# Decode attention: the cache pages of group B are loaded from ACT's queue, those of group A from SP's

## The chip, the cores and the metric

The kernel runs on one core of a Trainium2 chip. A core has TensorE (PE in the profile), VectorE (DVE), ScalarE (ACT), GpSimd (POOL) and SyncE (SP), each with its own stream of instructions, and 16 DMA engines that they share. Engines order themselves against each other by semaphores. The metric is the device time of one execution in microseconds. Before the change it is 2261.04 us, the median of 3 runs (2259.65 to 2265.12).

## The reference

One step of a hybrid decoder layer, for a prompt of 512 tokens and for 8 decode sequences of 4 new tokens each, with 4096 cached tokens per sequence in pages of 128. The input projection feeds three head groups: A (differential attention over a paged cache), B (sparse attention: compressed blocks, selected blocks, a window of 512) and C (matrix memory). What the change touches is the decode part of A and B, which reads the whole paged cache:

```python
past = (cache_a_kv[l][page_table].reshape(db, past_len, 2, H_A, HEAD),
        cache_b_kv[l][page_table].reshape(db, past_len, 4, DH_B), ...)
...
oa = diff_attention(qa, kv_a[:, :, 0].reshape(B, L, H_A, 2, DQ_A), kv_a[:, :, 1], q_pos, jnp.arange(L), lam)
...
kg = jax.vmap(lambda a, i: a[i])(ksb, idx).astype(jnp.float32)   # B: keys of the selected blocks
vg = jax.vmap(lambda a, i: a[i])(vsb, idx).astype(jnp.float32)   # B: their values
```

One page is 128 tokens. Of group A it holds 1024 floats per token (keys and values of 4 heads, 512 KB in all), of group B the kernel needs the 256 floats of k_sel and v_sel (128 KB). The table `page_table` says which of the 320 pages of the pool belong to a sequence, so the address of every load depends on a number that is read at run time.

## The kernel before

The program runs its stages one after the other: input projection, preparation, prompt attention, compressed branch, `decode_attend`, convolution, matrix memory, output projection. Each stage sets out its own instructions for each engine, fully unrolled in this one. The change is within `decode_attend` alone.

The stage works through 80 steps, 10 for each of the 8 sequences ("rows of the batch"). A step is `page` (4 cache pages, 512 tokens), `win` (the window of 512 cached rows) or `new` (the 4 fresh tokens). In a row they come as page 0, page 1, win, page 2, page 3, new, page 4 to page 7: 64 page steps in all. I call them P0 to P7, W and N. The four pages of a page step lie in one of four slots of the rings `pa` (group A) and `pb` (group B); page step m uses slot m % 4.

- SP, page step m: it waits until `summed` says that page step m - 4 has used its slot for the last time, reads four page numbers out of the table in SBUF into registers (L1214), and issues eight loads in turn, one of `pa` (L1218) and one of `pb` (L1220) for each page. All eight count up `loaded[m % 4]`; TensorE waits for 128 more on it. For a win step SP issues one load of 512 KB.
- TensorE is software pipelined over the steps. Its iteration n is: `score(n-1)` (keys times queries), `turn(n, 0)` and `turn(n, 1)` (transposes of the keys of heads 0 and 1 of step n into one of two PSUM buffers `tp`, L1296, the first behind the wait for the loads), `turn_p(n-2)`, the turns 2, 3 and 4 (the last is group B's), and `values(n-2)` (L1354, L1357), which counts up `summed`. A turn needs its `tp` buffer empty.
- ACT, iteration n: `copy_o(n-3)`, which waits for `summed` and copies the result of a step out of PSUM (L1460; L1462 for a win step, L1464 and L1465 for a new step), `copy_turn(n, 0)` (L1416, empties `tp`), `softmax(n-1)` (L1427, L1438), `copy_turn(n, 2)`, `copy_p(n-2)` (L1450), `copy_turn(n, 4)`. DVE empties the turns 1 and 3 (L1503).

So one iteration of ACT runs from one `copy_o` to the next, and TensorE's turns 2 and 4 can't start before ACT has emptied turn 0 and turn 2. The `copy_o` of step n-3 and SP's next loads are released by the same count of `summed`.

```python
for n in range(N + 9):
    if 3 <= n < N + 3:
        copy_o(n - 3)
    copy_turn(n, 0)
    if 1 <= n <= N:
        softmax(n - 1)
    copy_turn(n, 2)
    if 2 <= n < N + 2:
        copy_p(n - 2)
    copy_turn(n, 4)
```

Of the kernel before, what the change touches and what calls it, by code (L numbers as in the profile page):

```python
# [30 lines left out]
DB, DT = 8, 4  # L31
# [80 lines left out]
class Projection:  # L112
# [7 lines left out]
    PC, RING, NP = 2, 4, KC // 2  # L120
# [974 lines left out]
def decode_attend(nc, d, k):  # L1095
# [7 lines left out]
    NG, RING = PAGES // 4, 4  # L1103
# [17 lines left out]
    with Stage(nc, "da") as s:  # L1121
# [80 lines left out]
        with nc.Block() as block:  # L1202
            @block.sync
            def _(sp):
                sp.dma_start(table[:], d.page_table.rearrange("(a b) n -> a (b n)", a=1)).then_inc(table_loaded, 16)
                sp.wait_ge(table_loaded, 16)
                for n, (b, what, p) in enumerate(steps):
                    if what == "page":
                        m = b * NG + p
                        if m >= RING:  # L1210
                            old = next(x for x in range(N) if steps[x][1] == "page"
                                       and steps[x][0] * NG + steps[x][2] == m - RING)
                            sp.wait_ge(summed, old + 1)
                        _, pages = nc.values_load_multi_w_load_instructions(  # L1214
                            table[0:1, 4 * m:4 * m + 4], engines=[mybir.EngineType.SP],
                            min_val=0, max_val=d.cache_b.shape[0] - 1)
                        for i in range(4):
                            sp.dma_start(pa[:, m % RING, i, :], d.cache_a[bass.ds(pages[i], 1), :, :]  # L1218
                                         .rearrange("a p n -> p (a n)")).then_inc(loaded[m % RING], 16)
                            sp.dma_start(pb[:, m % RING, i, :], d.cache_b[bass.ds(pages[i], 1), :, 256:512]  # L1220
                                         .rearrange("a p n -> p (a n)")).then_inc(loaded[m % RING], 16)
                    elif what == "win":
                        if b >= 2:
                            sp.wait_ge(summed, n - 2 * G + 1)
                        sp.dma_start(pw[:, b % 2, :, :], d.b_win[b, :, :].rearrange(
                            "(i p) n -> p i n", p=P)).then_inc(win_loaded[b % 2], 16)
# [181 lines left out]
            def _(act):  # L1408
# [44 lines left out]
                def copy_o(n):  # L1453
# [11 lines left out]
                        last = act.activation(ob[:, b % 2, W0 + 1, :], po[:, 2 * HEAD:3 * HEAD], ACT.Copy)  # L1465
                    last.then_inc(o_copied, 1)

                act.wait_ge(consts_ready, 1)
                for n in range(N + 9):
                    if 3 <= n < N + 3:  # L1470
                        copy_o(n - 3)
                    copy_turn(n, 0)
                    if 1 <= n <= N:
                        softmax(n - 1)
# [1106 lines left out]
```

## Time and profile before

| What | Value |
|---|---|
| median of 3 runs | 2261.04 us |
| the profiled execution | 2258.08 us, its span 2256.4 us |
| busy in the span: PE, DVE, ACT | 78%, 38%, 26% |
| loads of group A's pages | x256, 512 KB each, 5.5 us from issue to landing (median) |
| loads of group B's pages | x256, 128 KB each, 5.9 us |
| read from HBM in all | 328.41 MB |

The page also shows the span in 40 slices. The decode stage fills the slices 20 to 28, the only ones in which the DMA engines stand at nine tenths without a break:

```
PE   7999999989999964986677777877516936018999
PEclk9999999999999985995899999999755655558999
DMA  5565555443333345000988999999201020631342
```

A digit is the busy share of a slice in tenths, 9 being 90% or more; PEclk is the clock that TensorE was granted, in tenths of full speed. One slice is 56.4 us. The chain of waits on the page follows only the end of the program, the output projection, so for this stage it says nothing: its rows are read from the trace, window by window.

### The profile page before, as it was taken

What the parts mean: (1) busy time and instruction counts of PE and PEld (TensorE: products, weight loads), DVE (VectorE), ACT (ScalarE), POOL (GpSimd) and SP (SyncE); (2) the same over time, 40 slices, a digit from 0 to 9 for tenths busy, and PEclk for the clock granted to TensorE, in tenths of its full rate; (3) what the DMA queues carried; (4) which work ended last, traced back from release to release, by engine and by line L of the source; (5) the groups of instructions that cost most, each with busy time, mean ns of one, the idle gap of its engine ahead of it and who ended that gap; (6) DMA issues with size and microseconds to landing.
All of it is one profiled execution on the core that took longest, in us unless ns stands there. A gap on an engine that the chain in (4) does not pass through costs nothing. (4 is left out here: it accounts for less than half of the span.)

```text
span 2256.4 us, 38647 instructions
## 1 busy us (share of the span) xinstructions
PE 1766.6 (78%) x14660; PEld 1381.5 (61%) x14660; DVE 860.6 (38%) x1568; ACT 597.0 (26%) x1273; POOL 120.1 (5%) x137
## 2 busy tenths in 40 slices
PE   7999989999999964986677777877516936018999
PEld 6888878888888853765465555555315633016777
DVE  4222212222222216762344555554573423493222
ACT  4221212121221214330344444444211200351111
POOL 2000000000000004000000000000000010350000
PEclk9999999999999985995899999999755655558999
DMA  5565555443333345000988999999201020631342
GB/s 187 181 194 173 184 172 180 158 130 109 103 114 103 106 142 196 30 29 20 357 326 316 330 332 341 329 352 329 91 13 47 19 55 15 214 118 62 118 131 80
DMA packets 213499, 365.64 MB, mean 162 GB/s; under 512 B 41662, under 2 KB 121087, under 8 KB 210919
## 3 DMA queue, kind: packets, MB, share of 16 engines
q1 hardware_dynamic: 212598, 360.51, 47.3%
q8 instruction: 113, 1.85, 0.3%
q10 hardware_dynamic: 288, 2.10, 0.2%
q0 software_dynamic: 432, 0.63, 0.2%
q14 instruction: 68, 0.55, 0.1%
HBM read 328.41 MB, written 39.02 MB: 163 GB/s over the span
## 5 line engine op out<-in xcount | busy, mean ns | idle before, releaser
L317 PE MATMUL pj_ps<-pj_whi,pj_xhi 128*128 128x512 f32 (+1 forms) x1024 | 402.3, 393 | 0.0
L318 PE MATMUL pj_ps<-pj_wlo,pj_xhi 128*128 128x512 f32 (+1 forms) x1024 | 395.2, 386 | 0.0
L319 PE MATMUL pj_ps<-pj_whi,pj_xlo 128*128 128x512 f32 (+1 forms) x1024 | 394.4, 385 | 0.0
L250 DVE TENSOR_TENSOR pj_wlo<-pj_w,pj_whi 128x1024 fp32r<-128x1024 f32 (+1 forms) x128 | 153.3, 1198 | 549.5 <-ACT pj_whi L222 546.5
L222 ACT ACTIVATE pj_whi<-pj_w 128x1024 fp32r<-128x1024 f32 (+1 forms) x128 | 132.7, 1037 | 542.4 <-DMA pj_w<-in_w_in 541.6
L317 PEld LDWEIGHTS pj_ps<-pj_whi,pj_xhi 128*128 128x128 f32 x1024 | 194.2, 190 | 48.8 <-issue 12.7
L319 PEld LDWEIGHTS pj_ps<-pj_whi,pj_xlo 128*128 128x128 f32 x1024 | 194.2, 190 | 38.2
L1296 PE MATMUL da_tp<-all_ident,da_pa 128*128 128x128 f32 x1024 | 155.9, 300 | 77.7 <-DMA da_pb<-in_cache_b_kv 76.0
L318 PEld LDWEIGHTS pj_ps<-pj_wlo,pj_xhi 128*128 128x128 f32 x1024 | 194.3, 190 | 35.4
L1416 ACT ACTIVATE da_kT<-da_tp 128x512 f32<-128x512 f32 x200 | 119.2, 596 | 261.3 <-PE da_tp L1296 261.1
L1296 PEld LDWEIGHTS da_tp<-all_ident,da_pa 128*128 128x128 f32 x1024 | 125.2, 153 | 99.2 <-DMA da_pb<-in_cache_b_kv 86.0
L1503 DVE COPY da_kT<-da_tp 128x512 f32<-128x512 f32 x128 | 88.5, 692 | 135.7 <-PE da_tp L1296 135.5
L2461 PE MATMUL ou_ps<-ou_whi,ou_mhi 128*128 128x512 f32 x256 | 101.6, 397 | 4.9 <-DVE ou_ms L2371 2.7
L2463 PE MATMUL ou_ps<-ou_whi,ou_mlo 128*128 128x512 f32 x256 | 100.7, 393 | 0.0
L2462 PE MATMUL ou_ps<-ou_wlo,ou_mhi 128*128 128x512 f32 x256 | 100.6, 393 | 0.0
L2445 PE MATMUL ou_ps<-all_ident,ou_att 128*128 128x128 f32 (+1 forms) x40 | 8.9, 401 | 109.8 <-DVE ou_hc L2405 109.8
L2376 DVE TENSOR_TENSOR ou_wlo<-ou_w,ou_whi 128x1024 fp32r<-128x1024 f32 x32 | 39.1, 1222 | 134.8 <-ACT ou_whi L2326 134.8
L1354 PE MATMUL da_po<-da_pa,da_pT 128*8 128x128 f32 x2048 | 68.2, 273 | 23.3 <-DVE da_pT L1551 12.1
L1518 DVE TENSOR_REDUCE da_nm<-da_sa 128x1 f32<-128x512 f32 x64 | 44.2, 691 | 92.5 <-PE da_sa L1310 92.5
L2445 PEld LDWEIGHTS ou_ps<-all_ident,ou_att 128*128 128x128 f32 (+1 forms) x40 | 7.2, 222 | 111.3 <-DVE ou_hc L2405 111.3
L2326 ACT ACTIVATE ou_whi<-ou_w 128x1024 fp32r<-128x1024 f32 x32 | 33.9, 1059 | 148.8 <-PE ou_ps L2467 141.0
L1354 PEld LDWEIGHTS da_po<-da_pa,da_pT 128*8 128x8 f32 x2048 | 49.9, 89 | 35.1 <-DVE da_pT L1551 26.7
(488 smaller groups left out, 2545.7 us busy)
## 6 DMA issues: line engine op xcount, KB each, us to landing
da_pa<-in_cache_a_kv SPq DMA_DIRECT2D x256, 512.0 KB, 5.5
pj_w<-in_w_in SPq DMA_DIRECT2D x120, 512.0 KB, 4.6
pj_pages<-in_cache_b_kv SPq DMA_DIRECT2D x256, 128.0 KB, 2.4
da_pb<-in_cache_b_kv SPq DMA_DIRECT2D x256, 128.0 KB, 5.9
ou_w<-in_w_out SPq DMA_DIRECT2D x32, 512.0 KB, 3.9
proj<-pj_out SPq DMA_DIRECT2D x60, 256.0 KB, 5.6
ap_rows_p<-proj SPq DMA_DIRECT2D x4, 1408.0 KB, 17.3
da_pw<-in_state_b_win SPq DMA_DIRECT2D x8, 512.0 KB
```

The lines of the kernel that those rows point to most:

```text
L222: act.activation(self.whi[:, g % self.RING, :, 0:n], self.w[:, g % self.RING, :, 0:n], ACT.Copy).then_inc(self.whi_ready, 1)
L250: dve.tensor_tensor(self.wlo[:, r, :, 0:n], self.w[:, r, :, 0:n], self.whi[:, r, :, 0:n], ALU.subtract).then_inc(self.wlo_ready, 1)
L317: pe.matmul(acc, hi, high, start=kc == 0, stop=False)
L318: pe.matmul(acc, hi, low, start=False, stop=False)
L319: last = pe.matmul(acc, lo, high, start=False, stop=kc == KC - 1)
L1296: last = pe.transpose(tp[at % 2][:, c, :], src, k.ident[:])
L1354: pe.matmul(po[32 * h:32 * h + 8, 0:HEAD], pT[:, n % 2, c, h, :], pa[:, r, c, 512 + HEAD * h:512 + HEAD * h + HEAD], start=(c == 0), stop= ...
L1416: act.activation(kT[:, n % 2, j, :].rearrange("p (c n) -> p c n", c=4), tp[at % 2][:], ACT.Copy).then_inc(act_copied, 1)
L1503: dve.tensor_copy(kT[:, n % 2, j, :].rearrange("p (c n) -> p c n", c=4), tp[at % 2][:]).then_inc(dve_copied, 1)
L2461: pe.matmul(ps[t][:], hi, wh, start=first, stop=False)
L2462: pe.matmul(ps[t][:], hi, wl, start=False, stop=False)
L2463: last = pe.matmul(ps[t][:], lo, wh, start=False, stop=end)
```

## The change

SP no longer issues the loads of `pb`. ACT has a new function `load_b(m)` that reads the four page numbers of page step m itself and issues the four loads of group B. ACT calls it for page steps 0 to 3 before anything else, and then in its main loop, right behind `copy_o` of a page step and ahead of `copy_turn(n, 0)`, for the page step four further on. It has no wait of its own: it stands behind `copy_o`, which waits for the same `summed`. Both engines count up the same semaphore `loaded[m % 4]`, so TensorE's wait is unchanged.

```diff
--- before.py
+++ after.py
@@ -1217,8 +1217,6 @@
                         for i in range(4):
                             sp.dma_start(pa[:, m % RING, i, :], d.cache_a[bass.ds(pages[i], 1), :, :]
                                          .rearrange("a p n -> p (a n)")).then_inc(loaded[m % RING], 16)
-                            sp.dma_start(pb[:, m % RING, i, :], d.cache_b[bass.ds(pages[i], 1), :, 256:512]
-                                         .rearrange("a p n -> p (a n)")).then_inc(loaded[m % RING], 16)
                     elif what == "win":
                         if b >= 2:
                             sp.wait_ge(summed, n - 2 * G + 1)
@@ -1465,10 +1463,25 @@
                         last = act.activation(ob[:, b % 2, W0 + 1, :], po[:, 2 * HEAD:3 * HEAD], ACT.Copy)
                     last.then_inc(o_copied, 1)
 
+                def load_b(m):
+
+                    _, pages = nc.values_load_multi_w_load_instructions(
+                        table[0:1, 4 * m:4 * m + 4], engines=[mybir.EngineType.Activation],
+                        min_val=0, max_val=d.cache_b.shape[0] - 1)
+                    for i in range(4):
+                        act.dma_start(pb[:, m % RING, i, :], d.cache_b[bass.ds(pages[i], 1), :, 256:512]
+                                      .rearrange("a p n -> p (a n)")).then_inc(loaded[m % RING], 16)
+
+                act.wait_ge(table_loaded, 16)
+                for m in range(RING):
+                    load_b(m)
                 act.wait_ge(consts_ready, 1)
                 for n in range(N + 9):
                     if 3 <= n < N + 3:
                         copy_o(n - 3)
+                        b, what, p = steps[n - 3]
+                        if what == "page" and b * NG + p + RING < DB * NG:
+                            load_b(b * NG + p + RING)
                     copy_turn(n, 0)
                     if 1 <= n <= N:
                         softmax(n - 1)
```

How the instructions of ACT stand before, from one `copy_o` of a page step to the next (L1416 empties a turn, L1427 and L1438 are the softmax, L1450 is `copy_p`):

```order
L1460 ACTIVATE da_ob<-da_po 128x2x128
L1416 ACTIVATE da_kT<-da_tp 128x512
L1427 ACTIVATE da_e,da_l<-da_sa,da_nm 128x512
L1438 ACTIVATE da_eb,da_l<-da_scores,da_nm 128x128
L1416 ACTIVATE da_kT<-da_tp 128x512
L1450 ACTIVATE da_pTb<-da_ptb 128x64
L1416 ACTIVATE da_kT<-da_tp 128x512
L1460 ACTIVATE da_ob<-da_po 128x2x128
```

And after, in the same place (the line numbers are lower by 2):

```order
L1458 ACTIVATE da_ob<-da_po 128x2x128
L1468 TENSOR_LOAD da_table
L1468 ISA x8
L1472 ISA
L1472 DMA da_pb<-in_cache_b_kv 128x256
L1472 ISA
L1472 DMA da_pb<-in_cache_b_kv 128x256
L1472 ISA
L1472 DMA da_pb<-in_cache_b_kv 128x256
L1472 ISA
L1472 DMA da_pb<-in_cache_b_kv 128x256
L1414 ACTIVATE da_kT<-da_tp 128x512
```

Ten rows have come in between `copy_o` and the first `copy_turn`: the read of the table, eight register instructions (ISA x8), and four loads, each with a register instruction ahead of it. All else on ACT stands in its old order.

SP's queue, one page step before (the first load pairs of it):

```order
L1214 TENSOR_LOAD da_table
L1214 ISA x8
L1218 ISA
L1218 DMA da_pa<-in_cache_a_kv 128x1024
L1220 ISA
L1220 DMA da_pb<-in_cache_b_kv 128x256
L1218 ISA
L1218 DMA da_pa<-in_cache_a_kv 128x1024
```

And after:

```order
L1214 TENSOR_LOAD da_table
L1214 ISA x8
L1218 ISA
L1218 DMA da_pa<-in_cache_a_kv 128x1024
L1218 ISA
L1218 DMA da_pa<-in_cache_a_kv 128x1024
```

SP still reads the page numbers, and four of its eight loads are gone from each page step. On TensorE, DVE and GpSimd nothing has moved.

## Rows read from the trace of the kernel before

**Rows 1.** Busy time by stretch, seven rows of the batch; columns stand in the first line
```profile
core 0: us, PE busy (x) PEld busy (x) DVE busy (x) ACT busy (x) POOL busy (x), PEclk, DMA share, GB/s
1109.15:1565.37 456.22, 351.75 (x5040) 266.83 (x5040) 220.12 (x499) 204.97 (x610) 0.00 (x0) 0.94 0.93 333
```

**Rows 2.** Who waited for whom in that stretch: us in total, times, longest us
```profile
PE da_tp L1296 <- DMA da_pb<-in_cache_b_kv: 67.3, 32, 5.2
PE da_tp L1296 <- ACT da_kT L1416: 14.7, 49, 0.4
ACT da_ob L1460 <- PE da_po L1357: 46.2, 56, 1.4
```

**Rows 3.** All copies of a step's result by ACT, page steps and window steps
```profile
L1460 ACT ACTIVATE da_ob<-da_po x64: 383/383/386, 1098.9 to 1600.7; 128x256 f32<-128x256 f32 x64
L1462 ACT ACTIVATE da_ob<-da_po x8: 272/272/277, 1109.2 to 1565.4; 128x128 f32<-128x128 f32 x8
```

**Rows 4.** Timeline, ACT and SP's queue, one window, page and late-token step: start us, us
```profile
1302.30 0.60 ACT L1416 ACTIVATE da_kT<-da_tp 128x512 f32<-128x512 f32 x1 [2.87 <-PE da_tp L1296]
1305.67 0.27 ACT L1462 ACTIVATE da_ob<-da_po 128x128 f32<-128x128 f32 x1
1310.47 0.38 ACT L1460 ACTIVATE da_ob<-da_po 128x256 f32<-128x256 f32 x1 [1.44 <-PE da_po L1357]
1311.25 0.60 ACT L1416 ACTIVATE da_kT<-da_tp 128x512 f32<-128x512 f32 x1 [0.40 <-PE da_tp L1296]
1311.97 0.33 SPq L1218 DMA_DIRECT2D da_pa<-in_cache_a_kv  x1
1312.50 0.33 SPq L1220 DMA_DIRECT2D da_pb<-in_cache_b_kv  x1
1315.25 0.38 ACT L1460 ACTIVATE da_ob<-da_po 128x256 f32<-128x256 f32 x1 [0.64 <-PE da_po L1357]
1316.88 0.60 ACT L1416 ACTIVATE da_kT<-da_tp 128x512 f32<-128x512 f32 x1 [1.25 <-PE da_tp L1296]
```

**Rows 5.** Timeline, ACT, pages without and with a wait, then a window step
```profile
1320.56 0.38 ACT L1464 ACTIVATE da_ob<-da_po 128x256 f32<-128x256 f32 x1 [0.20 <-PE da_po L1369]
1341.12 0.60 ACT L1416 ACTIVATE da_kT<-da_tp 128x512 f32<-128x512 f32 x1 [5.99 <-PE da_tp L1296]
1346.40 0.38 ACT L1460 ACTIVATE da_ob<-da_po 128x256 f32<-128x256 f32 x1 [0.64 <-PE da_po L1357]
1348.04 0.60 ACT L1416 ACTIVATE da_kT<-da_tp 128x512 f32<-128x512 f32 x1 [1.25 <-PE da_tp L1296]
...
1352.15 0.38 ACT L1460 ACTIVATE da_ob<-da_po 128x256 f32<-128x256 f32 x1 [0.64 <-PE da_po L1357]
1353.79 0.60 ACT L1416 ACTIVATE da_kT<-da_tp 128x512 f32<-128x512 f32 x1 [1.25 <-PE da_tp L1296]
1356.98 0.38 ACT L1460 ACTIVATE da_ob<-da_po 128x256 f32<-128x256 f32 x1 [1.44 <-PE da_po L1357]
```

**Rows 6.** Timeline, ACT, first row of the batch
```profile
1098.91 0.38 ACT L1460 ACTIVATE da_ob<-da_po 128x256 f32<-128x256 f32 x1 [1.44 <-PE da_po L1357]
```

**Rows 7.** SP's reading of page numbers and its issues: ns min/median/max, first and last start
```profile
L1214 SPq FUSED_REGOPS  x256: 147/152/160, 1071.6 to 1578.1; - x128
L1214 SPq SEQ_ASSERT  x256: 18/18/26, 1071.8 to 1578.3; - x128
L1214 SPq TENSOR_LOAD <-da_table x64: 293/298/483, 1071.1 to 1576.7; - x64
L1218 SPq DMA_DIRECT2D da_pa<-in_cache_a_kv x256: 332/333/1398, 1072.8 to 1581.7; - x128
```

**Rows 8.** The only issues that ACT makes, beside SP's two of the same line
```profile
L357 ACTq DMA_DIRECT2D pj_x<-in_x_prompt x2: 420/435/450, 0.8 to 1.3; - x2
L357 SPq DMA_DIRECT2D pj_x<-in_x_prompt x2: 384/403/422, 0.8 to 1.3; - x2
```

**Rows 9.** Busy time by stretch after a long wait of TensorE and later
```profile
1341.00:1346.00 5.00, 4.75 (x58) 4.34 (x60) 1.67 (x3) 2.95 (x8) 0.00 (x0) 0.74 1.03 376
1346.00:1352.00 6.00, 5.66 (x98) 4.42 (x93) 2.76 (x6) 3.23 (x9) 0.00 (x0) 1.00 0.63 173
```

## The prediction

> **What bounds the kernel now.** Only the decode stage is touched, so I leave the chain of waits, which lies in the output projection, and read the stage from three views.
>
> First the busy times by stretch. I take the stretch from the first copy of a window result to the eighth, 1109.15 to 1565.37 us, seven rows of the batch or 456.2 us, 65.17 us a row [rows 1, 3]. DMA is busy 0.93 of it at 333 GB/s, TensorE 351.75 us (0.77), ACT 205 us (0.45). No engine is full, though DMA nearly is: its work alone is 0.93 x 65.17 = 60.6 us a row.
>
> Second the waits. TensorE waited for page loads 67.3 us in all, but only 32 times for 56 page steps [rows 2]. In the other 24 page steps the load had landed, and TensorE's own chain with ACT and DVE set the pace. So the stage has two limits that lie close together: loads, and the loop TensorE - ACT - TensorE.
>
> Third the timeline of ACT, which gives that loop's length where no load was late. An ordinary page iteration: `copy_o` at 1346.40, first `copy_turn` at 1348.04, next `copy_o` at 1352.15 [rows 5]. That is 1.64 us in which TensorE scores and turns head 0, and then 4.11 us in which ACT and TensorE hand each other buffers. Sum 5.75 us. Eight of those would be 46 us; what lies between that and 65.17 us is W, N and the waits for loads.
>
> **The change part by part.**
>
> SP loses 4 of 8 issues for each page step, 4 x 0.52 us (start to start, 1311.97 to 1312.50) [rows 4]. I cost this at nothing. SP's own work was 1.50 us to the first issue and 8 x 0.52 us, 5.7 us of some 8, and the data of one 512 KB + 128 KB pair take 0.655 MB / 358 GB/s (333 / 0.93) = 1.8 us where the pair is issued in 1.05 us: DMA and not issuing sets when a page lands. The bytes are the same. The bounds of a gain from here are zero and the 7% of idle DMA, 4.6 us a row, 32 us in seven rows; that would need TensorE's loop to be short enough, which the next term excludes.
>
> ACT gains `load_b` 64 times, 4 of them ahead of the loop and 60 in it, 8 in each full row. What it takes I call L: the time from the start of `copy_o` until ACT can start `copy_turn(n, 0)`. From SP, which does the same work: `copy_o` at 1310.47 and SP's read are released by the same `summed`, and SP's first issue is at 1311.97, 1.50 us later; three more spacings of 0.52 us and the last issue's 0.33 us make 3.4 us [rows 4, 7]. For the hand-over to the next ACT instruction I add 0.25 us, and because ACT's only two issues took 0.435 us where SP's of the same line took 0.403 us [rows 8], 4 x 0.03 us. L = 3.75 us. The lower bound is the bare durations, 0.298 + 4 x 0.152 + 4 x 0.018 + 4 x 0.333 = 2.3 us [rows 7]; the upper 3.65 + 4 x 0.10 = 4.05 us if ACT's issues cost 0.435 us here too, and 4.3 us by a rival below. The row nearest is SP's own sequence, so 3.75.
>
> What does L push? Queued behind it are the first `copy_turn`, then the softmax, turn 2, `copy_p` and turn 4; TensorE's turns 2 and 4 and its `values` wait for them, and the next `copy_o`, and with it the next loads, wait for `values`. In that place ACT was idle anyway: 1.64 us in an ordinary page iteration, 0.78 us behind N or W, where scoring is short (1310.47 to 1311.25) [rows 4, 5]. So the hidden part is 1.64 or 0.78 us plus whatever wait for a load there was, and the rest of 3.75 us lengthens the loop.
>
> One row of the batch by iterations, `copy_o` to `copy_o`, loads never late. `load_b` stands in an iteration if the step three back is a page: that is all except those of N and P6.
> - N: 4.80 us (1305.67 to 1310.47), unchanged [rows 4]
> - P4: L + 4.00 (1311.25 to 1315.25); P2, behind W, the same: 2L + 8.00
> - P5: L + 3.68 (1316.88 to 1320.56) [rows 4, 5]
> - P6: 5.75, unchanged
> - P7, P0, P1: 3 (L + 4.11) = 3L + 12.33
> - W: L + 3.19 (1353.79 to 1356.98) [rows 5]
> - P3: L + 3.37 (1302.30 to 1305.67) [rows 4]
>
> Sum: 41.12 + 8L = 71.1 us at L = 3.75. DMA's 60.6 us a row is well below it, so waits for loads nearly vanish. The tight ones are P0 and P1: their slots come free one iteration and TensorE's scoring before they are due, 7.9 + 1.1 = 9.0 us (1.64 less the 0.5 us of the first transposes), and in the kernel before the last of eight loads landed 1.5 + 7 x 0.52 + 5.9 = 11.0 us after the release (5.9 us from the page's table of issues); the missing 2.0 us lie under L (3.75 - 1.64 = 2.1 us). I count nothing for them.
>
> The seven rows: 7 x (71.1 - 65.17) = +41.5 us. First row: from 1098.91 to 1109.15 us passed P2 and P3 [rows 3, 6], 10.24 us, which become 2L + 7.37 = 14.87: +4.6 us. Before that point the four opening calls keep ACT busy for some 4 x 3.75 = 15 us from 1071.1 us on [rows 7]; pages 0 to 3 are limited by DMA there, and I count nothing (bounds 0 and +3). Last row: only P4 and P5 have a `load_b`, +3.0 and +2.1 us, less the waits for loads that this covers: +3 (bounds 0 and 5). Behind the last copy at 1600.7 us [rows 3] nothing changes.
>
> Sum: 41.5 + 4.6 + 3 = +49 us. The profiled execution took 2258.08 us, so it would become 2307 us; the median of the runs shown lies 3.0 us above that execution, which gives 2310 us.
>
> **The rivals.**
>
> *Not slower: L is short or hidden.* 41.12 + 8L reaches today's 65.17 us at L = 3.0 us. If ACT's read and issues cost little more than their bare 2.3 us, the loop is 59.5 to 65 us and DMA's 60.6 us a row takes over again. Then the time is between no change and (65.17 - 62.5) x 7 = 19 us less, 2242 to 2268 us, with the middle at 2258. For it: spacings hold gaps (1.50 us for 0.98 us of work) that could be SP's own. Against it: nothing in the trace shows ACT's sequencer to be faster, and its two issues were slower than SP's.
> A second way to the same end is that ACT's sequencer starts `load_b` while `copy_o` still waits for `summed`. ACT idled 46.2 us before 56 such copies, 0.83 us each [rows 2], and L would shrink by at least that, to 2.9 us: no change. The Trainium skill's Perfetto Trace Analysis, DVE / Act Engine Instruction, speaks for it: the sequencer hands an ACTIVATE to a wait queue and takes the next instruction while the semaphore wait still runs. No row here shows an issue on ACT behind a waiting ACTIVATE. Both ways together: 0.17.
>
> *SP and ACT take turns at making descriptors.* Both start at the same `summed`, with the same 1.5 us of reading. If only one can issue at a time, a pair takes 2 x 0.33 = 0.66 us instead of 0.52, L grows by 4 x 0.14 = 0.6 us to 4.3 us, and 60 of these are +34 us: 2344 us. Against it: the two issues that ACT and SP began at 0.8 us took 0.42 to 0.45 and 0.38 to 0.42 us [rows 8]; one that had waited for the other would have taken twice its time. The Trainium skill's Perfetto Trace Analysis, DMA Instruction — HWDGE, states that one descriptor generator is shared and locked for each DMA; the trace agrees at most in part. 0.11.
>
> *TensorE's clock falls.* After a long wait for a load the granted clock was 0.74, and `copy_turn` to `copy_o` took 5.28 us (1341.12 to 1346.40) instead of 4.11; six microseconds later the clock was back at 1.00 [rows 5, 9]. TensorE's busy share would fall from 0.77 to about 0.70, but in short even gaps of 2 us instead of waits of up to 5.2 us [rows 2]. If the lower level held for half of the 80 iterations, 40 x 1.2 = +47 us: 2357 us. 0.08.
>
> **How the numbers follow.** The forecast, a slower kernel with ACT's loads in TensorE's loop, gets 0.64: 2310 us, its own range 2285 to 2338 (L 3.4 to 4.2, eight calls in 7.5 rows, 60 us per us of L). The case of not slower gets 0.17, turns 0.11, the clock 0.08. A measurement of this kernel tells about 0.3%, 7 us, from no change, so faster is below 2254 and slower above 2268. Of the 0.17, 0.07 is faster and 0.09 the same. The range 2264 to 2346 leaves out most of the not-slower case and the clock case.
>
> **What would show it.** Right: ACT issues x256 of `pb`, some 3.4 us from its read of the table to the end of the fourth issue; iterations of ACT of about 7.9 us between two `copy_o` of ordinary pages; TensorE's waits in `da_tp` change from the load (67 us) to ACT's `da_kT`; DMA share in the stage near 0.85. Wrong: `copy_turn` starting less than 3 us after `copy_o`, or waits for `pb` as long as before. If waits for loads stayed at 67 us and the loop grew as well, the two would add, and I would be too low.

## The result, and the profile after

The changed kernel takes 2373.93 us (median of 4 runs, 2370.21 to 2380.95), the kernel before beside it 2260.35 us (4 runs, 2250.43 to 2265.12): 1.051 times as long, 95% interval 1.047 to 1.056. The forecast was 2310 us in a range of 2264 to 2346. The direction was right, the size was not: 49 us were forecast and 113 came.

The profiled execution took 2370.21 us, 112 us more than the one before. The first question is where. The busy times by stretch, cut at the same places as before (from the first window result to the eighth, with the first row's part ahead and the last row's part behind):

```profile
core 0: us, PE busy (x) PEld busy (x) DVE busy (x) ACT busy (x) POOL busy (x), PEclk, DMA share, GB/s
1101.20:1116.80 15.60, 10.61 (x118) 7.17 (x110) 4.71 (x10) 5.83 (x17) 0.00 (x0) 0.89 0.81 291
1116.80:1672.20 555.40, 398.02 (x5040) 286.60 (x5040) 220.08 (x499) 204.84 (x611) 0.00 (x0) 0.87 0.75 273
1672.20:1714.00 41.80, 32.57 (x481) 22.86 (x481) 21.45 (x45) 16.89 (x54) 0.00 (x0) 0.90 0.43 151
```

The seven rows take 555.4 us where they took 456.2 [rows 1]: 79.3 us a row for 65.2, +99.2 us. The first part has 15.6 for 10.24 us (+5.4), the last 41.8 for 35.3 (1565.4 to 1600.7) [rows 3] (+6.5). That is all of the 112 us but 1. Two columns deserve a second look. TensorE's 5040 matmul records are the same number in both kernels, and they are busy for 398 us where it was 352: the same work takes 46 us more. And PEclk is 0.87 where it was 0.94.

Who waits, in that stretch (us in all, times, longest us), answers to [rows 2]:

```profile
PE da_tp L1294 <- ACT da_kT L1414: 97.3, 87, 3.2
PE da_po L1352 <- issue: 25.4, 7, 4.3
PE da_tp L1294 <- DMA da_pa<-in_cache_a_kv: 23.1, 12, 3.6
PE da_tp L1294 <- DMA da_pb<-in_cache_b_kv: 1.8, 1, 1.8
ACT da_ob L1458 <- PE da_po L1355: 60.9, 56, 2.5
```

TensorE's wait has changed hands, as forecast: 67.3 us for loads became 24.9, and 14.7 us for ACT's key copies became 97.3. The 25.4 us put down to "issue" are seven times in the window's step, where TensorE has no key turns left to do and stands before `values`, for which it needs ACT's and DVE's copies of the weights.

The page's table of issues, and what ACT's new instructions take (ns, min/median/max):

```profile
da_pb<-in_cache_b_kv ACTq DMA_DIRECT2D x256, 128.0 KB, 6.0
```

```profile
L1468 ACTq TENSOR_LOAD <-da_table x64: 304/308/503, 1070.5 to 1685.2; - x64
```

```profile
L1472 ACTq DMA_DIRECT2D da_pb<-in_cache_b_kv x256: 339/370/1528, 1072.1 to 1688.2; - x128
```

The timeline of ACT, two page steps with a load of group B, answers to [rows 5]:

```profile
1353.33 0.38 ACT L1458 ACTIVATE da_ob<-da_po 128x256 f32<-128x256 f32 x1 [1.44 <-PE da_po L1355]
1354.72 2.00 ACTq L1472 DMA_DIRECT2D da_pb<-in_cache_b_kv  x4
1356.82 0.60 ACT L1414 ACTIVATE da_kT<-da_tp 128x512 f32<-128x512 f32 x1 [3.10 <-issue]
...
1360.78 0.38 ACT L1458 ACTIVATE da_ob<-da_po 128x256 f32<-128x256 f32 x1 [0.64 <-PE da_po L1355]
1362.17 2.85 ACTq L1472 DMA_DIRECT2D da_pb<-in_cache_b_kv  x4
1365.12 0.60 ACT L1414 ACTIVATE da_kT<-da_tp 128x512 f32<-128x512 f32 x1 [3.96 <-issue]
```

From `copy_o` to the first `copy_turn` it is 3.5 us in the first and 4.3 in the second, where one of the four issues was held up. Over the 60 calls the fourth issue ends 3.75 us after the read began on average (median 3.62), and the next ACTIVATE starts at 3.92 (median 3.76). L was forecast as 3.75.

TensorE over the same kind of place, and its granted clock in stretches of 2 us:

```profile
1341.85 0.27 PE L1339 MATMUL da_ptb<-all_ident,da_eb 128*128 128x128 f32 x1
1344.59 1.09 PE L1294 MATMUL da_tp<-all_ident,da_pa 128*128 128x128 f32 x8 [2.47 <-ACT da_kT L1414]
1346.13 1.12 PE L1294 MATMUL da_tp<-all_ident,da_pb 128*128 128x128 f32 x4 [0.44 <-ACT da_kT L1414]
1347.17 0.63 PE L1359 MATMUL da_po<-da_pw,da_pTb 128*16 128x128 f32 x8
1347.93 1.82 PE L1308 MATMUL da_sa<-da_kT,at_qa 128*32 128x512 f32 x8
```

```profile
1342.00:1344.00 2.00, 0.12 (x2) 0.00 (x0) 0.74 (x2) 0.06 (x1) 0.00 (x0) 1.00 0.97 370
1344.00:1346.00 2.00, 1.09 (x8) 0.86 (x8) 0.28 (x1) 2.00 (x7) 0.00 (x0) 1.00 1.00 383
1346.00:1348.00 2.00, 1.75 (x16) 0.94 (x20) 1.25 (x7) 0.91 (x4) 0.00 (x0) 0.52 1.00 377
1348.00:1350.00 2.00, 2.00 (x17) 0.55 (x18) 0.10 (x1) 0.14 (x1) 0.00 (x0) 0.62 1.00 388
```

TensorE stands for 2.47 us, and when it is back at work the granted clock falls to the lower level (0.50 is 1.2 GHz, 1.00 is 2.4 GHz). The eight score matmuls of L1308, 1.04 us at the upper level, take 1.82. If PEclk is read as a mixture of the two levels, the seven rows hold (1 - 0.87) x 2 x 555 = 144 us at the lower one, where the kernel before held (1 - 0.94) x 2 x 456 = 55. The record of the clock has 35 falls in these rows, and 12 before.

What the level costs shows most clearly in P6, the page step without load code. These are two of its stretches from `copy_o` to the first `copy_turn`, with the same 22 matmul records and TensorE busy throughout:

```profile
1216.08:1217.85 1.77, 1.77 (x22) 0.97 (x19) 1.69 (x3) 0.55 (x2) 0.00 (x0) 1.00 1.02 399
1293.42:1296.73 3.31, 3.31 (x22) 1.61 (x20) 1.22 (x4) 0.55 (x3) 0.00 (x0) 0.50 0.56 217
```

Sorted by step, this is one row of the batch in us, means of the six full rows from the trace (each from P4 to the next row's N). "Shortest" is the shortest of the six second parts, and it agrees with the forecast's figure within 0.1 us in each line ([rows 4, 5]). The last column counts only time behind the first `copy_turn`:

| step | `copy_o` to first `copy_turn` | from there to next `copy_o` | shortest | of it at the lower clock |
|---|---|---|---|---|
| P2 | 3.86 | 4.88 | 3.93 | 2.8 |
| P3 | 3.77 | 3.83 | 3.37 | 1.6 |
| N | none | 5.52 | 4.80 | 2.1 |
| P4 | 3.61 | 4.57 | 3.97 | 1.4 |
| P5 | 3.98 | 4.40 | 3.67 | 2.2 |
| P6 | 2.80 | 4.43 | 4.12 | 0.7 |
| P7 | 3.83 | 4.85 | 4.12 | 1.9 |
| P0 | 4.06 | 4.28 | 4.12 | 0.4 |
| P1 | 4.47 | 4.87 | 4.12 | 1.9 |
| W | 3.82 | 3.71 | 3.20 | 1.2 |
| sum | 34.2 | 45.3 | 39.4 | 16 |

The forecast had 30.0 + 1.64 and 39.5 us: 71.1 in all. So of the 8.2 us a row that it missed, 1.4 are L in eight steps and 5.9 lie behind the first copy, where nearly every step that is longer than its shortest holds time at the lower clock. Another 1.2 are P6, which has no load code: in four of six rows its first part took 3.31 us, all of it at the lower clock, and in the other two 1.77. The three are 8.5, 0.3 more than the stretch gives, which has a seventh row. In all seven rows, 26 of the 70 second parts hold no time at the lower clock, and none of these is more than 0.07 us over its step's shortest. Of the 44 that hold some, 41 are over 0.1 us longer, and together they are 40.5 us longer. This is an attribution; the experiments below test it.

### The profile page after: what moved, and what is told of

The parts are those of the page before. It is cut to its first block and busy times, and to the rows that moved or that the text cites. A ratio compares the mean times of both kernels' runs of the same rounds, so it can differ in the third digit from the quotient of the medians.

```text
span 2368.4 us, 39225 instructions
## 1 busy us (share of the span) xinstructions
PE 1817.5 (77%) x14660; PEld 1401.5 (59%) x14660; DVE 860.5 (36%) x1568; ACT 596.8 (25%) x1273; POOL 120.1 (5%) x137
## 5 line engine op out<-in xcount | busy, mean ns | idle before, releaser
L1294 PE MATMUL da_tp<-all_ident,da_pa 128*128 128x128 f32 x1024 | 163.5, 311 | 122.6 <-ACT da_kT L1414 91.5
L1294 PEld LDWEIGHTS da_tp<-all_ident,da_pa 128*128 128x128 f32 x1024 | 131.3, 160 | 149.9 <-ACT da_kT L1414 103.7
L318 PEld LDWEIGHTS pj_ps<-pj_wlo,pj_xhi 128*128 128x128 f32 x1024 | 194.0, 189 | 35.3
L1352 PE MATMUL da_po<-da_pa,da_pT 128*8 128x128 f32 x2048 | 80.8, 308 | 38.1 <-issue 26.7
L1352 PEld LDWEIGHTS da_po<-da_pa,da_pT 128*8 128x8 f32 x2048 | 54.7, 98 | 57.3 <-issue 36.7
L1308 PE MATMUL da_sa<-da_kT,at_qa 128*32 128x512 f32 x512 | 80.0, 704 | 2.9 <-ACT da_kT L1414 2.1
```

Source lines behind the costliest of these rows:

```text
L318: pe.matmul(acc, hi, low, start=False, stop=False)
L1294: last = pe.transpose(tp[at % 2][:, c, :], src, k.ident[:])
L1352: pe.matmul(po[32 * h:32 * h + 8, 0:HEAD], pT[:, n % 2, c, h, :], pa[:, r, c, 512 + HEAD * h:512 + HEAD * h + HEAD], start=(c == 0), stop= ...
```

## The experiments

The first theory is this: ACT's own time between `copy_o` and the first key copy is the cost, and TensorE's clock, which falls in the gaps, multiplies it. Rivals: the second DMA queue itself; the clock as a mere companion of the lateness; loads that are late after all. Unless said otherwise a stretch is the seven rows between the first and the eighth window result. All runs, with the ratio to the kernel before (2251 to 2260 us beside them) and its 95% interval, and the stretch:

| kernel | us | ratio | stretch us | PEclk | TensorE waits for ACT's keys | for loads |
|---|---|---|---|---|---|---|
| before | 2260 | | 456.2 | 0.94 | 14.7 | 67.3 |
| changed | 2374 | 1.051 (1.047-1.056) | 555.4 | 0.87 | 97.3 | 24.9 |
| 14 idle reads | 2436 | 1.079 (1.075-1.083) | 613.4 | 0.83 | 135.8 | 12.5 |
| 12 idle reads | 2358 | 1.046 (1.043-1.049) | 546.2 | 0.88 | 89.3 | 36.2 |
| 7 idle reads | 2287 | 1.014 (1.012-1.017) | 477.6 | 0.95 | 62.0 | 30.3 |
| one issue | 2233 | 0.987 (0.984-0.991) | 425.9 | 0.97 | 15.5 | 46.6 |
| SP reads ahead, before | 2221 | 0.985 (0.981-0.989) | 415.0 | 0.98 | 16.2 | 38.9 |
| load behind the key copy | 2450 | 1.089 (1.084-1.094) | 627.9 | 0.82 | 157.3 | 6.6 |
| load before `copy_o` | 2363 | 1.048 (1.045-1.051) | 557.1 | 0.85 | 29.7 | 111.8 |
| ACT reads ahead | 2279 | 1.011 (1.006-1.016) | 465.0 | 0.94 | 58.8 | 26.3 |
| both read ahead | 2279 | 1.008 (1.005-1.011) | 471.8 | 0.95 | 62.7 | 26.0 |
| 20 fillers | 2434 | 1.077 (1.073-1.081) | 608.9 | 0.97 | 14.5 | 1.5 |
| 9 fillers | 2360 | 1.046 (1.043-1.050) | 549.1 | 0.94 | 35.3 | 20.5 |
| fillers in gaps | 2372 | 1.053 (1.049-1.058) | 550.0 | 0.97 | 49.2 | 21.7 |
| SP reads ahead, changed | 2350 | 1.040 (1.035-1.045) | 535.9 | 0.89 | 97.8 | 23.6 |
| the same, with fillers | 2346 | 1.038 (1.035-1.041) | 534.0 | 0.97 | 41.4 | 27.9 |
| the same, fewer fillers | 2341 | 1.037 (1.035-1.040) | 518.1 | 0.99 | 46.9 | 25.0 |

### ACT's time without the second queue

The kernel before, all loads on SP, with page numbers read on ACT that nobody uses (`...` stands for more code):

```
                        copy_o(n - 3)
+                       b, what, p = steps[n - 3]
+                       if what == "page" and b * NG + p + RING < DB * NG:
+                           nc.values_load_multi_w_load_instructions(
+                               table[0:1, 0:14], engines=[mybir.EngineType.Activation], ...)
```

> The kernel before, all loads on SP's queue, but ACT reads 14 page numbers into registers (about 0.3 + 14 x 0.23 = 3.5 us, used for nothing) in the 60 places where the change has load_b. Theory 1 (ACT's time in TensorE's loop is the cause, with the clock fall that follows from it): as slow as the changed kernel, 2360 to 2385 us, granted clock in the decode stage 0.86 to 0.89, no waits for loads to speak of. Theory 2 (the second DMA queue costs, by stalled issues and slower landings): about 2260 to 2310 us.

Measured: 2435.80 us, outside of the expected 2360 to 2385 because the reads took longer than planned. From `copy_o` to the first copy it was 4.5 us, and the loss is larger than the changed kernel's:

```profile
1118.00:1731.40 613.40, 427.28 (x5040) 297.33 (x5040) 219.75 (x499) 204.63 (x610) 0.00 (x0) 0.83 0.71 247
```

The whole picture is there without a single DMA on ACT: TensorE's wait for ACT, the low clock (5040 records, 427 us), the less busy DMA. The same with 7 and with 12 numbers:

> The kernel before, all loads on SP, with ACT reading 7 page numbers that nobody uses behind copy_o, where 14 of them (some 4.5 us from copy_o to the first copy's start) gave 2436 us. I expect about 2.2 us for 7. Slack theory (the first 1.25 us are hidden, as the idle time before the copy in the kernel before; the rest is priced like the rest of 14): 2259 + 176 x (2.2 - 1.25)/(4.5 - 1.25) = 2310 us; below 2300 if the shorter gaps leave TensorE's clock alone. Rival (proportional, no slack): 2345 us.

> The kernel before, all loads on SP, with ACT reading 12 page numbers that nobody uses behind copy_o: 0.23 us less for each of two reads than with 14, so 4.0 us from copy_o to the first copy, the changed kernel's mean of 3.9. Theory (ACT's time at that place is the whole of the change's cost, its second queue is neither good nor bad): the changed kernel's time, 2355-2390 us, with a granted clock of the stretch of 0.85-0.89. Rival (part of the 113 us is the second queue, the issues' own stalls or the two queues' order): 2335 us or less. Second rival (the second queue gains, and hides part of ACT's price): over 2395.

Measured: 2287.16 us with 7, where the copy came 2.6 to 2.9 us after `copy_o` except in P0 (5.9 to 7.1 us behind a late load), and 2358.22 us with 12, where it came at 3.58 us at the median and 3.89 on average. The second lies in its theory's range; the first is 23 us below the 2310, as was expected for a clock that the gaps leave alone:

```profile
1114.00:1591.60 477.60, 356.57 (x5040) 265.05 (x5040) 220.04 (x499) 204.03 (x610) 0.00 (x0) 0.95 0.88 317
```

```profile
1116.40:1662.60 546.20, 388.02 (x5040) 282.17 (x5040) 220.29 (x499) 205.47 (x611) 0.00 (x0) 0.88 0.79 277
```

So the place alone reproduces the change: a delay of 3.58 us (median; mean 3.89) costs 107 us (2358 for 2251 beside it), the changed kernel's 3.76 (mean 3.93) costs 113. And the price is not in proportion. The first 1 us beyond the 1.64 us that are free cost 33 us (2287 for 2254) and left the clock at 0.95; the next 0.9 us cost 74 us more, and the clock fell to 0.88.

### The second queue without ACT's time

The changed kernel, with one load of four neighbouring pages and no read (group B's data are then not those of the page table):

```
-                   _, pages = nc.values_load_multi_w_load_instructions(table[0:1, 4 * m:4 * m + 4], ...)
-                   for i in range(4):
-                       act.dma_start(pb[:, m % RING, i, :], d.cache_b[bass.ds(pages[i], 1), :, 256:512] ...
+                   act.dma_start(pb[:, m % RING, :, :], d.cache_b[4 * m:4 * m + 4, :, 256:512] ...
```

> The changed kernel with group B still on ACT's queue, but one load of the four pages from fixed neighbouring places of the cache, without reading page numbers (group B's pages are not those of the table). ACT's part shrinks from 3.8 us to about 0.6 us, which fits the 0.8 to 1.6 us in which ACT idled there. Theory 1: back to the kernel before, 2245 to 2275 us. Theory 2 (second queue): most of the 113 us stay, over 2320 us.

Measured: 2232.66 us, below the expectation and below the kernel before:

```profile
1111.60:1537.50 425.90, 341.56 (x5040) 257.41 (x5040) 219.57 (x499) 204.28 (x610) 0.00 (x0) 0.97 0.96 355
```

With one issue for each page step the second queue does no harm. It even frees something: with ACT out of the way DMA reaches 0.96 and 355 GB/s. The forecast's "SP's saving: nothing, bounds 0 and 32 us" held only because ACT's loop took the gain; here 30 us of stretch appear. Whether they come from SP's four fewer issues, from group B's earlier start or from the one load of neighbouring pages in place of four of scattered ones this run cannot tell.

### Where on ACT the loads stand

Two other places. Behind the first key copy:

```
                    if 3 <= n < N + 3:
                        copy_o(n - 3)
+                   copy_turn(n, 0)
+                   if 3 <= n < N + 3:
                        ...  load_b(b * NG + p + RING)
-                   copy_turn(n, 0)
```

And ahead of the next step's `copy_o`, where ACT waits for TensorE:

```
+                   if 4 <= n < N + 4:
+                       b, what, p = steps[n - 4]
+                       ...  load_b(b * NG + p + RING)
                    if 3 <= n < N + 3:
                        copy_o(n - 3)
-                       ...  load_b(b * NG + p + RING)
```

> The changed kernel with the load code behind the first key turn's copy and before the exponentials. The first copy is no longer late. Place theory: between the first copy and the third ACT had no idle time in the kernel before, so all 3.75 us of it push the third copy, on which TensorE's fifth turn waits: worse than the changed kernel, 2400-2460 us. Rival (only the way from copy_o to the first copy is on the path): 2270-2320 us.

> The changed kernel with the same reading and the same four issues on ACT, but placed before the wait of the next step's copy_o and not behind copy_o: there ACT waits some 1.1 us for TensorE anyway. Place theory (what counts is what of the 3.75 us sticks out of ACT's waits, here some 1.5 us where it was 2.5): 2285-2325 us, granted clock of the stretch above 0.90. Rival (group B's loads, now asked for one step, 7 to 8 us, later, hold TensorE up): 2370 us or more, with TensorE's wait for the loads over 60 us. Second rival (ACT's total work counts, wherever it stands): 2365-2385 us.

Measured: 2449.84 us behind the key copy, the worst of all, as expected: between the first and the second of its key copies ACT had nothing to wait for, so nothing of L is hidden. Ahead of `copy_o` 2362.76 us, which my theory missed by nearly 40 us; it lies below both rivals' ranges too, but with the waits for loads that the first rival named. ACT's keys were nearly in time there, its copies of the weights not, and the loads now started a step later, so that TensorE waited for them most:

```profile
PE da_tp L1294 <- DMA da_pb<-in_cache_b_kv: 111.8, 28, 8.0
PE da_tp L1294 <- ACT da_kT L1414: 29.7, 56, 2.2
PE da_po L1352 <- ACT da_pTb L1448: 28.8, 14, 2.7
```

Here the load that is partly hidden on ACT is late for TensorE. Neither of the two places is free both ways.

What can be moved is the reading of the numbers, which needs no slot:

```
+                       pages = read_b(b * NG + p + RING) if ahead else None
                        copy_o(n - 3)
+                       if ahead:
+                           load_b(b * NG + p + RING, pages)
```

> The changed kernel with ACT reading the four page numbers ahead of its wait in copy_o and only the four issues behind copy_o. The read takes 1.4 of the 3.9 us, and ACT waits there for 0.6 to 1.4 us anyway, so copy_o to the first copy falls to 2.5-2.9 us. Place theory, by the kernel with 7 idle reads (2.6 to 2.9 us, 2287 us): 2275-2300 us, granted clock 0.93 or more. Rival (every instruction on ACT costs its time wherever it stands, or the issues themselves are the burden): 2345-2375.

Measured: 2279.45 us, as expected. Three quarters of the loss are gone with four issues of DMA still on ACT:

```profile
1335.69 0.39 ACT L1458 ACTIVATE da_ob<-da_po 128x256 f32<-128x256 f32 x1 [0.72 <-PE da_po L1355]
1336.15 1.86 ACTq L1473 DMA_DIRECT2D da_pb<-in_cache_b_kv  x4
1338.11 0.60 ACT L1414 ACTIVATE da_kT<-da_tp 128x512 f32<-128x512 f32 x1 [2.03 <-PE da_tp L1294]
```

The first issue comes 0.46 us after the start of `copy_o` in this step and 0.16 us at the median of the 60, where it came 1.39 us after it (1353.33 to 1354.72), and the key copy here comes at 2.4 us. This settles a rival of the forecast too. Had ACT's sequencer run the read while `copy_o` waited 1.44 us for TensorE, the order of the code would not have mattered.

### How early the loads start

SP's four numbers read ahead of its wait for the slot, in the kernel before:

```
                        m = b * NG + p
+                       _, pages = nc.values_load_multi_w_load_instructions(...)
                        if m >= RING:
                            ...
                            sp.wait_ge(summed, old + 1)
-                       _, pages = nc.values_load_multi_w_load_instructions(...)
```

> The kernel before, with SP's reading of the page numbers ahead of its wait for the free slot instead of behind it. The first load starts 1.5 us earlier after each release. Theory 1 sees DMA idle 7% of the stage, 4.6 us a row, by late releases: 10 to 25 us faster, 2236 to 2251 us. If TensorE's own loop sets the pace, no change.

Measured: 2221.21 us, 38 us less than the kernel before where 10 to 25 were expected, and the fastest of all:

```profile
1109.40:1524.40 415.00, 337.29 (x5040) 252.59 (x5040) 219.45 (x499) 204.19 (x611) 0.00 (x0) 0.98 0.99 365
```

DMA is at 0.99: what bounded the kernel before beside TensorE's loop was the time from a slot's release to the first issue. The same edit in the changed kernel, and in the one in which ACT reads ahead as well:

> The changed kernel, with SP reading its four page numbers ahead of its wait for the slot, which was worth 38 us in the kernel before: group A's loads start 1.4 us sooner. In the changed kernel TensorE still waits 23.1 us for group A's loads in the 555 us of the stretch, and 1.8 for group B's. Theory (ACT's lateness and the low clock hold the rest, late loads are a small part): 2345-2372 us. Rival (the loads that I took to be early again are what is missing in my sum): 2335 us or less.

> The changed kernel, with SP and ACT both reading page numbers ahead of their waits (2279 us with ACT alone doing so). The first key copy is still 0.7 to 1.0 us later than in the kernel before, but the loads come 1.4 us sooner on both queues, which was worth 38 us on one: 2235-2260 us. Rival (the second queue is the better way to load once ACT's time is small): under 2221 us, the time of the kernel before with reading ahead on SP.

Measured: 2350.08 us (2374 without), in its theory's range, and 2278.65 us, which is outside of the expected 2235 to 2260: where ACT reads ahead, SP's reading ahead brings nothing more (2279.45 without it). TensorE's waits for loads change hands instead. Without SP's reading ahead the load that comes last is group A's, with it mostly group B's, from ACT's queue, and the sum stays:

```profile
PE da_tp L1294 <- DMA da_pa<-in_cache_a_kv: 26.3, 12, 3.8
```

```profile
PE da_tp L1294 <- DMA da_pb<-in_cache_b_kv: 19.9, 9, 3.2
PE da_tp L1294 <- DMA da_pa<-in_cache_a_kv: 6.1, 3, 3.3
```

The rival, that two queues beat one, fell with it: 2279 against 2221 us.

### TensorE's clock

Fillers are matmuls of 128x128 on the identity, written to a score buffer that is free at the time. They occupy TensorE where it would wait for ACT, and change no result:

```
                    if n >= 2:
                        turn_p(n - 2)
+                   if 3 <= n < N and steps[n - 3][1] == "page" and own > 2:
+                       done = ...
+                       for i in range(20):          # 9 in the second kernel
+                           pe.matmul(sa[done % 2][:, 0:P], k.ident[:], k.ident[:], start=True, stop=True)
                    for x in range(2, own):
```

> The changed kernel with 20 matmuls of 128x128, whose results nobody reads, on TensorE between turn_p and turn 2, where it waits about 2.5 us for ACT. If the fall of the granted clock from 0.94 to 0.87 makes the part that the forecast missed, the clock goes back to 0.95 or more and the time to 2310 to 2330 us, the forecast's. If the clock only comes along, the time stays at 2365 to 2385 us or grows by the fillers' length.

Measured: 2433.52 us. The clock came back to 0.97, but the fillers took twice the gap, so the run tells nothing of the price (each filler leaves two records):

```profile
1345.16 4.63 PE L1388 MATMUL da_sa<-all_ident 128*128 128x128 f32 x40
```

> The changed kernel, with 9 filler matmuls of 128x128 on TensorE between the turn of the weights and the third key turn, in the steps in which ACT makes a group B load; 20 of them took 4.6 us, so 9 take about 2.1 us and lie inside the 2.3 to 2.5 us for which TensorE waits there. Clock theory (part of the lost time is TensorE at its lower level after such gaps): the granted clock of the stretch goes from 0.87 to 0.95 or more, and the time falls from 2374 to 2315-2345 us although TensorE has more to do. Rival (ACT's lateness is the whole of it, the clock only follows): the clock rises likewise, the time stays at 2365-2390 us.

Measured: 2360.04 us. Neither theory's range. Clock 0.94, but the stretch only 6 us shorter:

```profile
1118.00:1667.10 549.10, 455.17 (x5922) 369.23 (x5922) 220.22 (x499) 204.75 (x611) 0.00 (x0) 0.94 0.78 276
```

By steps the theory is there: P3 to P7 go back to their shortest times (3.38, 4.80, 3.97, 3.68, 4.12, 4.15 us in the second part). But P0 went from 4.3 to 6.8 us. There a load came late, and the fillers stood behind the late load instead of in a gap. I tried to take them out of that step, and took them out of the wrong one (the test named the step behind the window, P2), with 24 in the window's step:

> The changed kernel with fillers only where TensorE has a gap: 9 in the page steps other than the one behind the window (where the run before showed them to cost time), and 24 in the window's own step, in which that run still had TensorE idle for 4.3 us. Clock theory, from that run: without low clock each step behind the first key copy takes its shortest time, 39.4 us a row in all, and with copy_o to copy at 31.4 + 1.8 us this is 72.6 us a row where the changed kernel has 79.3: 7 x 6.7 = 47 us less, 2325 us (2310-2340), granted clock of the stretch 0.97 or more. Rival (the clock only follows ACT's lateness, and the 14 us of the run before are all there is): 2350-2375.

Measured: 2371.50 us, the rival's range. P3 to P7 are at their shortest again, P2 is back at 5.1 us with 2.8 us of low clock, and P0 takes 6.1 us. TensorE in P0:

```profile
1235.43 1.09 PE L1294 MATMUL da_tp<-all_ident,da_pa 128*128 128x128 f32 x8 [1.67 <-DMA da_pb<-in_cache_b_kv]
...
1236.90 2.17 PE L1388 MATMUL da_sa<-all_ident 128*128 128x128 f32 x18
1238.91 1.04 PE L1294 MATMUL da_tp<-all_ident,da_pa 128*128 128x128 f32 x8
```

TensorE had waited for the load already; ACT's key copy, ready at about 1237.6 us, would have let the next turns start before the fillers were done.

Next, the loads' lateness was taken down first (the kernel in which SP reads ahead, 2350 us), and fillers were put in outside P0, then outside P0 and P1:

> As the last, with fillers on TensorE in its gaps: 9 in page steps, 14 in the window's step, none in the step of a batch's first page, where they came behind a late load before. Clock theory (about 40 us of the stretch are the low clock): granted clock 0.95 or more and at least 25 us less than the last kernel, 2315-2340 us. Rival (without the low clock the loads are late again and take the gain, the two are in one loop): within 12 us of the last kernel.

> As the last kernel with fillers (534.0 us of stretch, 2346 us), without them in the step of a batch's second page too, where they stood behind a load that came late, so that their 2.2 us were paid in full in each of eight rows. Clock theory: the other steps stay at their shortest time, and this one goes from 7.6 to 4.4-5.4 us behind its first copy as without fillers: 2.2 to 3.2 us a row, 2318-2332 us, at a granted clock of the stretch of 0.95 or more. That would be 18 to 32 us for the clock alone, against 2350 us for the same kernel without fillers. Rival (the gaps and the loads take it back whatever the clock does): 2340-2355 us.

Measured: 2346.03 us, the rival's range, and 2340.60 us (2337.86 to 2342.65). The stretches, without fillers, with, and with fewer:

```profile
1118.70:1654.60 535.90, 381.86 (x5040) 275.92 (x5040) 219.89 (x499) 204.48 (x611) 0.00 (x0) 0.89 0.79 283
```

```profile
1117.50:1651.50 534.00, 452.61 (x5992) 368.51 (x5992) 219.90 (x499) 204.67 (x611) 0.00 (x0) 0.97 0.80 283
```

```profile
1115.90:1634.00 518.10, 430.87 (x5866) 345.68 (x5866) 219.59 (x499) 203.80 (x610) 0.00 (x0) 0.99 0.83 292
```

In the profiles the last one is 17.8 us shorter over the seven rows than the one without fillers; in the medians it is 9.5 us, with intervals that overlap (1.035 to 1.040 against 1.035 to 1.045), and 2340.6 lies at the edge of the rival's range and outside of mine. So the medians alone don't show that the clock has a price. The parts of the stretch do: without fillers the second parts are 43.5 us a row and P6's first part 2.43, some 33 us over their shortest in seven rows; with the fewer fillers they are 40.0 and 1.77, and 28.6 of the 33 us have come back. But the first parts of the eight steps with load code grew from 3.83 to 4.02 us on average, which takes 10.8 us. Of these 0.19 us, 0.15 lie within ACT's own code, whose issues are held up longer, and the rest behind it. At a clock of 0.99 the forecast's formula holds with the L of that kernel: 41.12 + 8 x 4.02 = 73.3 us a row, measured 518.1 / 7 = 74.0.

## Why the prediction was wrong in size

**Right: what ends last.** ACT's load code in TensorE's loop was the mechanism, not the second queue. The delay without the queue reproduces the loss (2358 us at a mean of 3.89 us, the changed kernel's 2374 at 3.93), the queue with little delay is faster than before (2233 us).

**Right: L.** Forecast 3.75 us, measured 3.9 on average. It was read from SP doing the same work. The difference is in issues that are held up (32 of the 60 calls have an issue over 0.6 us, up to 1.53 in the row of L1472), and in the late loads of P0 and P1. Eight calls make 1.4 us a row, 10 us over the seven.

**Right in kind: the loads.** "Waits for loads nearly vanish" was too much. 67.3 us became 24.9, and "I count nothing for them" left out what remained, above all in P0 and P1, whose first copies come at 4.06 and 4.47 us.

**Wrong: the step that failed is the sum of a row, 41.12 + 8L.** Its constant was put together from intervals at the upper clock, so the sum puts the lower level at nothing. The clock was priced on top of it only in a rival, 2357 us at 0.08, and the range ended at 2346, below that. The reason given was that short even gaps would spare the clock. They did not: the fall comes with the longer loop. In the steps where no load is late (P2 to P5, P7) the calls make gaps of mostly 1.4 to 2.9 us in front of TensorE, in the window's step of 3.6 us on average, and part of these gaps is followed by time at the lower level. PEclk went from 0.94 to 0.87, the same 5040 records from 352 to 398 us, and the part of a row behind the first copy from 39.4 to 45.3 us. Over seven rows these 5.9 us a row and the 1.0 us of P6 (2.80 for 1.77) are 48 of the 57.7 us that the sum missed (99.2 less 41.5), close to the 46 us that TensorE's records are longer; L is 10. The rival's price, +47 us for half of the iterations, was near to what the traces show. Taken into the sum, it would have given 2357 us; the other 17 us up to 2374 are mainly L and the ends of the stage. The first row was right (+5.4 for +4.6), the last too small (+6.5 for +3): PEclk is 0.90 there, where it was 1.00 before.

**What stays open.** The runs do not separate the clock's share cleanly. Restored from 0.89 to 0.99 by fillers it gave 18 us of stretch in the profiles and 9.5 us in the medians, and not the 33 us that the same reading gives for that kernel, because longer first parts took back 11. For the changed kernel, with its 48 us, no run restores the clock without other costs. In a loop in which late keys, late loads and a low clock each leave room for the others, taking away one uncovers the next; the shares above are those of the changed kernel's trace and not what each would give back. The kernels with idle reads show the same without fillers: 33 us for the first microsecond, with the clock at 0.95, and 74 for the second, with 0.88.

**The rivals.** *Not slower* (0.17): it needed L under 3.0 us or a sequencer that reads ahead by itself. L was 3.9, and only the rewritten order brought it down, to 2.4 us in the step shown. The Trainium skill's Perfetto Trace Analysis, DVE / Act Engine Instruction, has the sequencer take the next instruction while an ACTIVATE waits. The trace differs, and decides: in all 60 calls `copy_o` had waited 0.47 to 2.48 us, and the read of the table started 5 to 7 ns after `copy_o` did, never before it. The issues came 1.39 us behind its start; only the order of the code brought them forward, to 0.46 us in the step shown. *Taking turns* (0.11): a queue that waits for the other would have given 4.3 us in every call; the median was 3.76, and single issues of up to 1.5 us are held up, not all of them by 0.14 us. Such issues don't need a second queue either: in the kernel before, 32 of SP's 450 issues in the stretch took over 0.6 us,

```profile
L1220 SPq DMA_DIRECT2D da_pb<-in_cache_b_kv x256: 332/333/1542, 1073.4 to 1582.3; - x128
```

but with two queues they are more frequent, 37 of SP's 224 and 34 of ACT's 224. The Trainium skill's Perfetto Trace Analysis, DMA Instruction — HWDGE, states a shared generator that is locked for each DMA; the held-up issues agree with it at most in part, and no run isolated them.

## What to carry to other kernels

A DMA issue or a table read on a compute engine is an instruction in that engine's order: cost it from the row of the queue that does it today, and lay it against the idle time in front of the very next instruction, not against the engine's idle share (ACT was 45% busy here). When a forecast makes a gap in front of TensorE longer, the clock is a term of the same sum and not only a rival: put the lower level's price on the intervals behind the new gaps. And before moving work to a second queue, look at what lies between a slot's release and the first issue. Reading the page numbers ahead of the wait, on the one queue, gave 38 us, more than any arrangement with two that was tried.

## What the runs showed of the hardware that was not expected

- Gaps of 0.4 to 1.6 us in front of TensorE, beside a longer wait for a load in P0 and one of 2.4 us in the window's step (7 idle reads, first key copy mostly 2.6 to 2.9 us after `copy_o`), left the granted clock at 0.95; gaps of mostly 1.4 to 2.9 us (the changed kernel) brought it to 0.87, and in the place shown it fell when TensorE was back at work, not in the gap.
- An issue on ACT took 0.37 us at the median, but up to 1.53 us in a stretch in which DMA was busy 0.75 of the time; 32 of 60 groups of four held one over 0.6 us.
- On ACT a read of the table behind a waiting `copy_o` did not start before it: 5 to 7 ns after its start in all 60 calls.
- Reading page numbers on ACT is not cheap: 1.39 us from `copy_o` to the first issue with four numbers. The table read itself took about 0.31 us with 4 numbers, 1.23 with 14, 0.78 with 12 and 0.96 with 7, so its time does not simply grow with their count:

```profile
L1475 ACTq TENSOR_LOAD <-da_table x60: 1218/1230/1431, 1099.5 to 1746.8; - x60
```

```profile
L1475 ACTq TENSOR_LOAD <-da_table x60: 781/784/982, 1099.8 to 1675.7; - x60
```
